# Dilated layer's past: the whole-row tiles in another order of rows, sixteen groups of eight rows 64 KB apart

## The reference, cut to what matters

```python
idx = q_idx[:, None] - d * jnp.arange(span + 1)[None, :]
kg = k_all[:, idx]
vg = v_all[:, idx]
s = jnp.einsum('nqhd,nqkhd->nqhk', q, kg).astype(f32) * ATTN_SCALE
pr = jnp.exp(s - m[..., None])
den = jnp.sum(pr, axis=-1)
o = jnp.einsum('nqhk,nqkhd->nqhd', pr, vg.astype(f32)) / den[..., None]
...
wt = den * jnp.exp(m - jnp.max(m, axis=0))
return jnp.sum(wt[..., None] * o, axis=0) / jnp.sum(wt, axis=0)[..., None]
```

## Time and profile before

| what | value |
|---|---|
| median of 3 runs | 2652.58 us (2648.06 to 2653.84) |
| span of the profiled execution, first to last instruction | 2628.4 us |
| its own time outside the profile | not given apart; the median stands 24.2 us over the span |
| TensorE, VectorE, ScalarE, GpSimd busy | 86%, 55%, 33%, 13% |
| mean granted TensorE clock | 0.911 of full speed |
| read from HBM | 378 MB |
| the dilated layer's past | from about 1811 to 2117 us |

### The profile page before, as it was taken

How to read it: one execution, slowest core, us unless ns; L and a number is a source line. 1 busy time by engine, 2 the same in 40 slices (tenths; PEclk the granted TensorE clock), 3 DMA queues, 4 the chain that set the end, 5 groups by cost and what they waited for, 6 DMA issues and landing times. The chain is left out here.

```text
span 2628.4 us, 63413 instructions
## 1 busy us (share of the span) xinstructions
PE 2264.2 (86%) x26373; PEld 1765.9 (67%) x26373; DVE 1440.4 (55%) x2317; ACT 872.6 (33%) x1577; POOL 342.1 (13%) x434
## 2 busy tenths in 40 slices
PE   6788888888978987799999989997777776999998
PEld 3566777776737864577777757655666654777776
DVE  2436788885565546654422365476666657453223
ACT  2335444442231222333312221165333323333222
POOL 2003233331000000111100000033111110111000
PEclk8898899998978987899999989998878888999999
DMA  7323899995250034123233224444999921332331
GB/s 251 107 81 124 282 380 381 375 379 189 74 192 19 4 105 132 56 73 89 80 97 89 88 79 138 145 129 111 267 288 278 277 82 39 91 88 81 89 89 61
DMA packets 306664, 392.62 MB, mean 149 GB/s; under 512 B 23680, under 2 KB 224714, under 8 KB 306404
## 3 DMA queue, kind: packets, MB, share of 16 engines
q1 hardware_dynamic: 276580, 282.15, 35.0%
q0 software_dynamic: 29824, 106.71, 12.4%
HBM read 378.11 MB, written 10.70 MB: 148 GB/s over the span
## 5 line engine op out<-in xcount | busy, mean ns | idle before, releaser
L836 PE MATMUL bank<-yT,WH 128*128 128x288 f16 x3200 | 533.0, 290 | 45.9 <-DVE yT L690 34.6
L836 PEld LDWEIGHTS bank<-yT,WH 128*128 128x128 f16 x3200 | 314.2, 99 | 144.8 <-issue 48.8
L900 DVE SCALAR_TENSOR_TENSOR WL<-wring,WH 128x1024 f16<-128x1024 f32 x194 | 255.1, 1319 | 258.4 <-ACT WH L880 258.3
L1383 DVE TENSOR_TENSOR KL<-bank,KH 128x512 f16<-128x512 f32 x416 | 281.0, 687 | 174.5 <-ACT KH L1363 166.2
L1363 ACT CAST KH<-bank 128x512 f16<-128x512 f32 x416 | 242.3, 584 | 360.5 <-PE bank L1281 358.5
L836 PE MATMUL bank<-uT,WH 128*128 128x288 f16 x2048 | 338.2, 288 | 10.6 <-DVE WL L900 10.6
L836 PE MATMUL bank<-yT,WL 128*128 128x288 f16 x1600 | 331.8, 290 | 0.0
L880 ACT ACTIVATE WH<-wring 128x1024 f16<-128x1024 f32 x194 | 203.5, 1054 | 266.2 <-PE bank L836 221.4
L836 PEld LDWEIGHTS bank<-uT,WH 128*128 128x128 f16 x2048 | 201.6, 99 | 63.4 <-DVE WL L900 11.2
L836 PE MATMUL bank<-uT,WL 128*128 128x288 f16 x1024 | 210.9, 288 | 0.0
L836 PE MATMUL bank<-hT,WH 128*128 128x288 f16 x960 | 164.0, 295 | 29.1 <-DVE hT L727 18.7
(11 more groups left out here) (457 smaller groups left out, 3967.9 us busy)
## 6 DMA issues: line engine op xcount, KB each, us to landing
wring<-in_ada_w SPq DMA_DIRECT2D x96, 512.0 KB, 4.6
vTd<-in_state_dil_k SPq DMA_DIRECT2D x80, 512.0 KB, 12.7
vslot<-in_state_dil_v POOLq DMA_DIRECT2D x78, 512.0 KB, 12.8
yT<-in_cache_fox_k SPq DMA_DIRECT2D x128, 256.0 KB
krows<-in_cache_fox_k SPq DMA_DIRECT2D x128, 256.0 KB
wring<-in_mlp_up SPq DMA_DIRECT2D x64, 512.0 KB, 4.1
wring<-in_mlp_down SPq DMA_DIRECT2D x64, 512.0 KB, 3.9
wring<-in_ev_w_in SPq DMA_DIRECT2D x26, 512.0 KB, 3.8
```

The costliest lines, as they stand in the source:

```text
L836: last = nc.tensor.matmul(bank[b + h][:, 0:HALF], w[s % 2][:, c, :], x[:, s % parts * KC + c, h * HALF:(h + 1) * HALF], start=(s % parts = ...
L900: nc.vector.scalar_tensor_tensor(WL[s % 2][:, :, :], w[:, :, :], WSCALE, WH[s % 2][:, :, :], ALU.mult, ALU.subtract).then_inc(w_free, 1)
L1383: nc.vector.tensor_tensor(KL[i][:, :], turned[n % NT][:, :], KH[i][:, :], ALU.subtract).then_inc(lo_out, 1)
```

## The change

The partitions of the whole-row tiles hold their 128 rows in another order. Before, partition p holds row p of the tile. After, the partitions form 16 groups g of eight, and the r-th partition of group g holds row 16 r + g. `dilated_keys` follows, so the constant `lc_past` holds its values in the new order.

```diff
@@ def dilated_keys():
     early = (np.arange(96)[:, None] * 16 + np.arange(8)[None, :]).reshape(6, P)
-    return np.concatenate([early, 1536 + np.arange(512).reshape(4, P)])
+    late = 1536 + np.arange(512).reshape(4, 8, 16).transpose(0, 2, 1).reshape(4, P)
+    return np.concatenate([early, late])
@@ def load_tile(name): ... def load(eng, n, dst, done):
                     if tile < 6:
                         a = early[seq:seq + 1, tile * 16:(tile + 1) * 16, 0:8, :].rearrange("a g r n -> (a g) r n")
                     else:
-                        a = src[seq:seq + 1, 1536 + (tile - 6) * P:1536 + (tile - 5) * P, :].rearrange("a w n -> (a w) n")
+                        a = src[seq:seq + 1, 1536 + (tile - 6) * P:1536 + (tile - 5) * P, :].rearrange("a (r g) n -> (a g) r n", g=16)
                     eng.dma_start(dst[:, :], a).then_inc(done, 16)
```

## The result

The changed kernel takes 2662.76 us in the median of 20 runs (2642.42 to 2682.31), the kernel before 2649.3 us (20 runs, 2636.11 to 2658.2). The ratio is 1.0055, 95% interval 1.0037 to 1.0073: slower by 0.55%, some 14.6 us. The prediction was 2662 and slower. Two of the 20 runs of the changed kernel, 2682.2 and 2682.31 us, count as slow ones and are left out of the ratio.

What follows compares the result with a forecast made beforehand. The prediction took the full DMA queues of the dilated layer's past as the bound; +8.2 us for the main stretch and +1.4 for the start, sum +9.6, on the median 2652.6 gave 2662 us, range 2634 to 2694.

Steps and rivals of the forecast that it cites:

- What bounds the stage: Dilated layer's past: always-full DMA queues set the pace, 281 GB/s at share 1.02 from 1860 to 2108 us.
- Form against addresses: Dilated past tiles: the form of 16 groups of 8, likelier than memory distances, is slow, so whole-row tiles become slow.
- a mixed stretch at the pace of the slow stream: Dilated stage, one stream grouped and one plain: 270 GB/s, near the slow kind's 277, not the middle, 317.
- Rival A: Dilated past: addresses are slow, the new order mends it; mixed stretches reach 317 GB/s, -18 us, 2634; chance 0.15.
- Issue, bias table: SP's K issues 6.5 us longer in all, hidden behind TensorE; bias constants reordered in the same shape, nothing.
- The rate: Dilated stage, 1860 to 2108 us: 69.7 MB at 272 GB/s take 256.2 us, +8.2; whole sum +9.6 us.
- all-part traffic: K and V both moving tiles of eight rows of every sixteen: 272 GB/s, weighted from 277 steady and 237 at start.
- the steady stretches: Seven stretches, 79 us, of the dilated stage with both streams grouped: mean 277 GB/s, from 258 to 293.
- The first part: Start of the dilated stage: 1825 to 1839 us at 272 GB/s, +1.4 us; 1839 to 1860, queues dry, nothing.
- The time around the span: Start and end around the profiled span of 2628.4 us, taken as 24.2 us from the median of 2652.6.
- Rival C: Dilated past: streams stay in step, the start's 237 GB/s becomes the rule; +50 us, 2702, half way +25; chance 0.12.
- The signs: Dilated stage: SP's issues near 536 ns, 400 GB/s peaks gone, 250 to 290 throughout, sequences about 1.2 us longer.

Runs made afterwards that it cites:

- e3: Kernel before with all ten past tiles of a sequence in the plain form 128x1024 (some late positions left out, others read twice): ratio 0.9761.
- e1: Changed kernel's grouped form, but whole-row tiles keep neighbouring rows in each group, groups 9 rows apart: ratio 1.0063 against the kernel before.
- e7: Kernel before with K in ten plain tiles and V unchanged (outputs of the sample group wrong): ratio 0.9923.
- e2: Kernel before with eight of ten tiles in plain form, rows 64 KB apart, the last two grouped, all keys kept: ratio 0.9866.
- e6: e3 with each tile sent as two plain transfers, the even partitions and the odd ones: ratio 0.979 against the kernel before.
- e8: e2 with the last two tiles each sent as four plain transfers of every fourth partition: ratio 0.9823 against the kernel before.
- e5: e3 with each tile sent as two plain transfers, partitions 0 to 63 and 64 to 127: ratio 1.0114 against the kernel before.
- e4: Kernel before with every tile read as 128 rows of two 2 KB pieces from two sequences, form 128x2x512: ratio 0.9784.

## Why the prediction came out as it did

**What bounds the stage.** Right. The DMA share stayed at 1.03 while the rate fell, and e3, which does the same work between its all-reduces in 180 us instead of 223 (before) and 239 (changed), shows that nothing else was near at 223 us: TensorE was busy 152 of its 180 us.

**Form against addresses.** Right, and now shown from both sides: the form with other addresses is as slow as the change (e1), the addresses with a plain form are fast (e3). The argument that decided it, a mixed stretch at the pace of the slow stream, is shown by e7's slices. Rival A had a chance of 0.15 and no run speaks for it. Why the form is slow is not shown.

**Issue, bias table.** Both at nothing, and nothing was seen: SP's issues are 536 ns, and SP waited 229 us for TensorE between them.

**The rate.** Here is the term that was mis-sized. I took 272 GB/s for all-part traffic, the mean of the steady stretches and the start. Between the all-reduces it was 263, for 69.7 MB 265 us instead of the 256.2 of the sum, +17 where I had +8.2. The first part had +1.4 in the sum, from 14 us at 272, and nothing from 1839 to 1860, where the queues of the kernel before run dry. In the changed kernel the start went at 233 until 1866 with the queues full (DMA share 0.99), and from the first V tile to the second all-reduce it is 75.0 us before and 81.6 after, +6.6. I had gone below the steady mean of 277 because those stretches came after fast or mixed ones; it should have been further. Whether that reason is the right one no run tests, and that such a stretch spreads the engines no run shows; what was measured is 263 GB/s between the all-reduces and 233 at the start. The profiled pair gives 23.4 us, the medians 13.5 and the ratio 14.6, against +9.6. The median agrees with 2662 closer than the working deserves, and that is luck: the median shown before had been 2652.6 of three runs, that of 20 is 2649.3, and this makes up for most of the small sum.

**The time around the span.** A plain error: I called 24.2 us "start and end around" the span. It is 1.8 us, and the profiled execution of the kernel before was a short one. It did no harm because the sum was added to the median, but rates read from it may be on the good side, which goes the same way as the error of the rate.

**Rival C.** It was a part of the truth. From 1827 to 1866 us the rate was 232, 39 us instead of the 12 of the kernel before, and from 1874 to 1905 it was 245 where the kernel before had 283 (1860 to 1885); only then did it come to 263, and it wasn't 237 for good.

**The signs.** SP's issues and the lost peaks came as said. The steady flow was to be 250 to 290 GB/s and had 263 in the mean, with many slices under 250; a sequence was to be 1.2 us longer and was 2.8 us longer in the profiled pair, a sixth of 16.7 us.

## What to carry to other kernels

When a stage keeps the DMA queues full, cut its windows by the form of the transfers under way and compare the rates, before asking about addresses. In this stage a tile of 128 partitions moved fast where its slowest dimension was 128 with one uniform step (345 GB/s with all tiles so in e3, against 263 with all of them as 16 groups of 8 in the changed kernel): try to reorder what a partition holds until that is so, as e2 does for eight tiles of ten (302 GB/s), even if the rows come from 64 KB apart. Where a transfer has fewer partitions, try every second or fourth (e6 342 GB/s, e8 315) before neighbours (e5 266). One stream of the slow kind slowed the good one beside it (271 GB/s for both in e7): K alone gained 0.8% (e7), both 2.4% (e3); and the two executions that you have profiles of can differ by more than the change, here by 36 us against 14.6.

## What the hardware showed that I had not expected

Plain transfers of 64 neighbouring partitions cost as much as the grouped form: 266 GB/s (e5) beside 263 in the changed kernel, against 342 for even and odd partitions (e6). Three dimensions with 2 KB pieces cost little, 332 against 345 GB/s (e4, e3). And beside one grouped stream a plain one gained nothing: 271 GB/s for both together over 24 us (e7).
